# Moving the buffers of a four-layer matmul kernel to other SBUF addresses

## The reference, cut to what matters

```python
proj = h @ w_in                 # layer 1: 1024 x 10240, layer 2: 1024 x 4096
return y @ w_out                # 1024 x 1024
proj = x @ w_in                 # hybrid mixers: 1024 x 7256
merged @ w_out + b_out
u = x @ w_up                    # 1024 x 5632
(jax.nn.gelu(a) * b) @ w_down   # 2816 x 1024
```

## The kernel before

| buffer | start, byte | start modulo 512 |
|---|---|---|
| UT | 16512 | 128 |
| WS, and each slot and part in it | 49280 + 8192 n | 128 |
| WR | 98432 | 128 |
| CT | 114816 | 128 |
| SM | 118464 | 192 |
| AT, AF | 121536 | 192 |
| AR | 154304 | 192 |
| EX, EA | 205504 | 192 |
| MF | 222912 | 192 |

## Time and profile before

### The profile page before, as it was taken

One profiled execution on the slowest core, in us unless ns is written; L12 is line 12 of the kernel. 1 busy time (PEld: TensorE's weight loads), 2 busy tenths in 40 slices (PEclk: granted clock), 3 DMA queues, 4 the chain that ended last, 5 costly groups with the idle time before them and its releaser, 6 DMA issues.

```text
span 2716.8 us, 36054 instructions
## 1 busy us (share of the span) xinstructions
PE 2677.7 (99%) x13721; PEld 2153.6 (79%) x13721; DVE 1219.1 (45%) x2468; ACT 1049.5 (39%) x2005; POOL 1139.0 (42%) x894
## 2 busy tenths in 40 slices
PE   8999999999999999999999999999999999999998
PEld 6888888897778877776788888887777678888887
DVE  4434334443555456544246424265644423642426
ACT  3333434443446343452333424234445333342422
POOL 4434344435342443333365444444333336444443
PEclk9999999999999999999999999999999999999999
DMA  6444343432331332224252333324222425233331
GB/s 191 130 116 124 98 125 97 130 125 86 109 94 55 112 97 78 78 82 134 100 182 72 116 93 95 99 79 130 81 68 88 136 93 175 83 118 100 93 93 63
DMA packets 215056, 286.39 MB, mean 105 GB/s; under 512 B 16862, under 2 KB 154562, under 8 KB 214116
## 3 DMA queue, kind: packets, MB, share of 16 engines
q1 hardware_dynamic: 214884, 284.08, 34.2%
HBM read 248.31 MB, written 18.94 MB: 98 GB/s over the span
## 4 chain that ended last, share of the span: by engine, by line
PE 96%; DVE 2%; ACT 1%; POOL 1%; issue 1%; DMA 0%; ACTq 0%; DVEq 0%; POOLq 0%
PE banks L1687 39%; PE banks L1684 29%; PE banks L1680 13%; PE banks L1818 2%; PE banks L1705 2%; PE banks L1744 1%; PE banks L1800 1%; PE banks L1904 1%; PE banks L1720 1%; PE banks L1927 1%; PE banks L1839 1%; PE banks L1977 1%; PE banks L1861 1%; PE banks L1890 1%; PE banks L1786 1%; PE banks L1915 1%
## 5 line engine op out<-in xcount | busy, mean ns | idle before, releaser
L2991 POOL TENSOR_TENSOR WS<-WR,WS 128x512 fp32r<-128x512 f32 (+2 forms) x676 | 856.3, 1300 | 1048.6 <-ACT WS L2040 1048.6
L1687 PE MATMUL banks<-WS,UT 128*128 128x512 f32 (+1 forms) x3696 | 797.0, 365 | 3.9 <-DVE UT L2393 3.9
L1687 PEld LDWEIGHTS banks<-WS,UT 128*128 128x128 f32 x3696 | 605.8, 190 | 131.4 <-issue 36.4
L1684 PE MATMUL banks<-UT,WS 128*128 128x512 f32 (+1 forms) x2832 | 660.8, 392 | 0.7 <-ACT AR L2222 0.7
L1684 PEld LDWEIGHTS banks<-UT,WS 128*128 128x128 f32 (+1 forms) x2832 | 526.0, 187 | 125.8 <-issue 16.0
L2040 ACT ACTIVATE WS<-WR 128x1024 fp32r<-128x1024 f32 (+1 forms) x344 | 333.1, 1018 | 221.4 <-PE banks L1687 144.3
L1680 PE MATMUL banks<-UT,WS 128*128 128x512 f32 x1536 | 371.1, 395 | 0.0
L1680 PEld LDWEIGHTS banks<-UT,WS 128*128 128x128 f32 x1536 | 282.5, 188 | 61.9 <-issue 4.9
L1687 PE MATMUL banks<-WS,AT 128*128 128x512 f32 x1296 | 308.5, 396 | 0.0
L1687 PEld LDWEIGHTS banks<-WS,AT 128*128 128x128 f32 x1296 | 242.4, 188 | 58.2 <-ACT WS L2040 0.7
L2989 POOL TENSOR_TENSOR WS<-WR,WS 128x512 fp32r<-128x512 f32 x128 | 177.9, 1422 | 251.6 <-ACT WS L2036 251.6
(11 more groups left out here) (226 smaller groups left out, 2665.2 us busy)
## 6 DMA issues: line engine op xcount, KB each, us to landing
WR<-in_w_in SPq DMA_DIRECT2D x112, 512.0 KB, 3.6
WR<-in_w_up SPq DMA_DIRECT2D x88, 512.0 KB, 3.5
WR<-in_dil_w_in SPq DMA_DIRECT2D x64, 512.0 KB, 3.8
WR<-in_w_down SPq DMA_DIRECT2D x40, 512.0 KB, 3.7
WR<-in_diff_w_in SPq DMA_DIRECT2D x32, 512.0 KB, 3.8
WR<-in_dil_w_in SPq DMA_DIRECT2D x32, 256.0 KB, 3.2
AR<-AF SPq DMA_DIRECT2D x128, 64.0 KB, 2.3
AR<-AF SPq DMA_DIRECT2D x64, 128.0 KB, 2.4
```

Source lines behind the costliest of these rows:

```text
L1684: mm = pe.matmul(B[bank][0:c, :], w[part][:, kk, g * P:g * P + c], act[:, other, kk, :], start=start, stop=stop)
L1687: mm = pe.matmul(B[bank][:, off:off + n], act[:, other, before_k + kk, g * P:g * P + P], w[part][:, kk, :], start=start, stop=stop)
L2991: ge.tensor_tensor(slot(i, 1)[:, s], raw(i)[:, s], slot(i, 0)[:, s].bitcast(F32), ALU.subtract).then_inc(lo_p.sem, 1)
```

## The change

Four things move; no instruction is added, removed or reordered.

1. The slots of `WS` grow from 4096 to 4096 + 128 elements (512 bytes more).
2. The arena with `AT`, `AR`, `MF` and `EX` comes directly behind `WR`, ahead of `CT` and `SM`. `AR` starts 128 elements later behind `AT` than before, and shrinks from 17152 to 17008 elements (its last tables, `oSIN` and `oCOS`, move down by 144).
3. `slot` adds `lead(i)` to the start of a tile: 112 elements (448 bytes) for `l1w?`, `l1g?` and `l2g?`, 16 elements (64 bytes) for `f?a0`, `f?b0` and `f?b10`, and 0 for all others.
4. Tiles in `AT` are addressed through `AW`, the same bytes with 16 elements more.

| buffer | start after, byte | start modulo 512 before | after |
|---|---|---|---|
| UT, WR | 16512, 99968 | 128 | 128 |
| WS slots | 49280 + 16896 n | 128 | 128 |
| WS, tiles l1w, l1g, l2g | 448 further | 128 | 64 |
| WS, tiles f?b10 | 64 further | 128 | 192 |
| AT and AF | 116352 | 192 | 128 |
| AT, tiles f?a0 and f?b0 | 64 further | 192 | 192 |
| AR | 149632 | 192 | 128 |
| EX, EA | 200832 | 192 | 128 |
| MF | 217664 | 192 | 64 |
| CT | 222304 | 128 | 96 |
| SM | 225952 | 192 | 160 |

```diff
-        WS = sb("WS", [P, NS, 2, KC * 256], F32R)
+        WS = sb("WS", [P, NS, 4096 + 128], F32R)
         WR = sb("WR", [P, 2, KC * 256])
+
+        AR_LEN, EXT = 17008, 12800
+        o_ar = 4 * (8192 + 128)
+        base = -(-nc.sbuf_base // 32) * 32
+        sb("arena", [P, 8192 + 128 + AR_LEN + 1152 + 8])
         CT = sb("CT", [P, C_TAB])
         SM = sb("SM", [P, 768])
-
-        base = -(-nc.sbuf_base // 32) * 32
-        sb("arena", [P, 8192 + 17152 + 1152 + 8])
-        EXT = 12800
         AT = nc.alloc_sbuf_tensor_at("AT", [P, 2, KC, T], F32R, offset=base)
+        AW = nc.alloc_sbuf_tensor_at("AW", [P, 2 * KC * T + 16], F32R, offset=base)
         AF = nc.alloc_sbuf_tensor_at("AF", [P, 2 * KC * T], F32, offset=base)
-        AR = nc.alloc_sbuf_tensor_at("AR", [P, 17152], F32, offset=base + 32768)
-        MF = nc.alloc_sbuf_tensor_at("MF", [P, 1152], F32, offset=base + 32768 + 68608)
-        EX = nc.alloc_sbuf_tensor_at("EX", [P, 2, KC * 256], F32R, offset=base + 32768 + 4 * EXT)
-        EA = nc.alloc_sbuf_tensor_at("EA", [P, 2, 4, T], F32R, offset=base + 32768 + 4 * EXT)
+        AR = nc.alloc_sbuf_tensor_at("AR", [P, AR_LEN], F32, offset=base + o_ar)
+        MF = nc.alloc_sbuf_tensor_at("MF", [P, 1152], F32, offset=base + o_ar + 4 * AR_LEN)
+        EX = nc.alloc_sbuf_tensor_at("EX", [P, 2, KC * 256], F32R, offset=base + o_ar + 4 * EXT)
+        EA = nc.alloc_sbuf_tensor_at("EA", [P, 2, 4, T], F32R, offset=base + o_ar + 4 * EXT)
...
-        oSIN, oCOS = 17088, 17120
+        oSIN, oCOS = 16944, 16976
...
+        def lead(i):
+            name = tiles[i][0]
+            if name[:3] in ("l1w", "l1g", "l2g"):
+                return 112
+            return 16 if place[i] > NS or name[2:] == "b10" else 0
+
         def slot(i, part):
             _, k, n, _ = tiles[i]
             s = place[i]
+            o = 2048 * part + lead(i)
             if s < NS:
-                return WS[:, s, part, 0:k * n]
+                return WS[:, s, o:o + k * n]
             if s > NS:
-                return AT[:, s - NS - 1].rearrange("p k t -> p (k t)")[:, part * 2048:part * 2048 + k * n]
+                o += 4096 * (s - NS - 1)
+                return AW[:, o:o + k * n]
             return EX[:, part, 0:k * n]
```

## The result

| | before | after |
|---|---|---|
| median, 6 runs each | 2717.52 us (2716.45 to 2718.52) | 2708.11 us (2705.81 to 2709.33) |
| profiled execution (span) | 2718.07 us (2716.8) | 2707.59 us (2706.3) |
| mean granted clock in it | 0.999 | 0.998 |

The ratio of the times is 0.9963, with a 95% interval of 0.9952 to 0.9974: the change gains 9.4 us, where 16.0 us were forecast. Lines of the changed kernel are 12 further than those of the earlier trace rows: 1687 is 1699, 1684 is 1696, 1680 is 1692, 1705 is 1717, 1720 is 1732.

What follows compares the result with a forecast made beforehand. TensorE's matmul spacings were taken to bound the kernel, a matmul running in 99% of the span. Gains of 5.1, 3.1, 1.4, 0.5, 4.7 and 1.2 summed to 16.0 us, predicting 2701.4 us, range 2697.5 to 2709.5.

Steps and rivals of the forecast that it cites:

- d: Moving operand's start minus the stationary one's, modulo 512 bytes; claimed to set matmul spacing: 512 columns 226.7 ns at 0, 233.3 at -64.
- addresses do nothing: Rival for the whole kernel: the paces come from something other than operand place, time stays 2717.4 us; chance 0.05.
- (a): Four pieces of 192 matmuls (f?d0, f?d1), WS moving, AT stationary: 233.3 to 226.7 ns each, gaining 5.1 us.
- (b): Output projections of layers 1 and 2 and last down projection, AT stationary, WS or EX moving: gain of 3.1 us.
- (d): 96 matmuls with EX moving and UT stationary go from d = +64 to 0: gain of 0.5 us.
- (c): Line 1684 with AT or EA moving, 576 matmuls, goes from d = +64 to 0: gain of 1.4 us.
- (e): Tiles l1w, l1g, l2g, 1152 matmuls of 256 columns, go from d = 0 to -64: gain of 4.7 us.
- (f): Tiles f?b10, 192 matmuls of line 1720, take the pace of line 1705: gain of 1.2 us.
- (g): Tiles f?a0 and f?b0 keep their pair of starts, 128 and 192, so nothing changes.
- its rival, that the tiles gain nothing: Start values, not d, decide for l1w, l1g, l2g: 2706.1 us, or 2713 with mirrored loss; chance 0.12.
- (h): About 890 transposes go from d = -64 to -32: taken as 0, ends 4 us loss and 1 us gain.
- (i): Other engines keep their work and none bounds; TensorE gains at most 6% in a stretch; no time counted.

Runs made afterwards that it cites:

- scan1: Matmul-only kernel, not the reference: 16 differences of operand start in steps of 32 bytes; 512 columns took 226.7 ns at d = 0, 233.3 at -64.
- scan3: Matmul-only kernel with stationary operands of 128, 64 and 32 columns, either operand moved; 512 columns at d = 0 took 226.7, 230.0 and 231.6 ns.
- scan4: Matmul-only kernel: both operands shifted together, loads of 16 columns and 1 column, moving start in 16-byte steps; 226.65 ns unshifted, 239.4 shifted 4 bytes.
- arena_only: Changed kernel without the leads for l1w, l1g, l2g and f?b10; 2710.42 us, ratio 0.9976 to the kernel before.
- d76: Changed kernel with tables starting at 64 modulo 512 and leads making d = -76 for tiles used with 256 columns; 2712.86 us, ratio 0.9983.
- scan2: Matmul-only kernel: 64 differences of operand start, -128 to +124 bytes in steps of 4; 512 columns took 226.7 to about 240.3 ns.

## Why the prediction was right and wrong

**What bounds the kernel, and that d separates the pairs: right.** `scan1` shows both paces with no other engine at work, and that at 512 columns the difference and not the values decides on the 64-byte grid. The rival "addresses do nothing" is out, and with it, for these matmuls, the rule of the Trainium skill, "SBUF — State Buffer", section "Who interferes with whom", that "PE and ACT never wait on anyone", as far as TensorE's two own reads are concerned: 226.7 against 233.3 ns and -8.1 us in the kernel. The other rule that the prediction quoted, "TensorE: Matmul & The Clock Gate", section "Step-by-step: what each phase is for", by which the load takes nothing from the stream, is not borne out either: in `scan3` what d = -64 costs falls from 6.7 to 2.7 ns with a load half as wide, and in `scan4`, with a load of one column, the stationary start no longer counts. That only bits below 512 count was right for the steady pace at 512 columns, and too wide: on the 64-byte grid 256 is enough.

**(a) and (b), 8.2 us forecast, -8.1 us measured in `WS`,`AT`.** The size was right; one piece of the working in (b) was not. `EX` and `AT` both started at 192 before, so the 144 matmuls of that pair had d = 0 already and had nothing to gain. It cost nothing in the sum, since the short pieces gained 5.7 ns each (528 matmuls, 3.0 us) where I had allowed 2.9. The reading behind that allowance was wrong too: the piece of 96 at 1411 us had 229.6 ns not for being short but for the pair of part (d) in it, and had 21.77/96 = 226.8 ns after the change. Two errors cancelled here.

**(c) and (d), right**: -1.3 and -0.4 us for 1.4 and 0.5.

**(e), (f) and (g): here the main step failed, in that d = -64 at 256 columns was given one pace.** It has two, 117.8 and 113.3 ns, and a run keeps the one with which it begins. The trace of before showed it, in a row that I didn't use: the first run of line 1705 in the same view as the earlier trace rows, 24 matmuls, stood at 117.9 ns.

```profile
1457.12 2.83 PE banks L1705 x24
```

I read the pace off the two runs of 48 and gave it to `l1w0` ("10.9 us as well"), to `f?b10` ("exactly the pair of line 1705") and to line 1705 itself ("Nothing"). Measured: `l1w0` 11.31 us for 96, `f?b10` 22.61/192 = 117.8 ns, and both 48s of line 1717 flipped from the fast pace to the slow one, +0.8 us. That is the sign of being wrong that the prediction had named, a changed pace of a pair whose d did not change. (e) came to 3.7 of 4.7 us: the 96 of `l1w0` gained 2.1 ns each, the 732 matmuls in runs of 12 2.6 ns, and those in runs of 24 to 60 4.4 to 6.2 ns; 0.9 of the 3.7 us came without the leads (`arena_only`). (f) came to 0.4 of 1.2; (g) to -0.8 of 0. Together 2.6 us of the shortfall. Neither bound of (e) was reached, and its rival, that the tiles gain nothing, fell: the leads alone gave -2.9 us.

**(h), right.** Eight transposes still take 0.87 us; `scan1` has 109.2 ns at every d. Both rivals by which the transposes themselves pay are out. What comes behind them did pay: line 1717's flip stands in `arena_only`, which moved their operands.

**(i), wrong in kind, small in size.** "TensorE gains at most 6% in a stretch" was no argument against a wait, because this stage had no slack at all: from the first matmul of `f?b10` to the late tile it takes 18.6 us in seven kernels. The prediction looked at TensorE's longest waits alone; the weight loads' idle time of 0.7 us behind "ACT WS" stood in the trace of before. It does name that sign. The wait costs what `f?b10` gained, 0.3 of 0.4 us here and 1.2 of 1.2 us in `d76`. So (f) was worth nothing however fast it became.

**Not in the sum**: one more stretch of half clock, 1.7 us, and 0.7 us of other waits. The six executions give 2705.81 us at a mean clock of 0.999 and up to 2709.33 at 0.997. The clock varies from execution to execution, but a mean of 0.998 or less was more frequent with moved addresses (28 of 55 executions, against 5 of 44 of the kernel before), so it is not scatter alone, and the forecast had no term for it.

**The time and its range.** The median, 2708.11 us, lies 6.7 us above the forecast and within the range of 2697.5 to 2709.5 us. That is partly luck: the high end was made for gate tiles that gain nothing and transposes that pay, and neither came. Two paces at one d, the wait and the clock filled the room in their place, and none of them had a price in the forecast.

In all, by the rows of the table of groups: 16.0 forecast, less 0.3 in (a) to (d), 1.0 (e), 0.8 (f), 0.8 (g), 0.3 (the wait), 1.7 (clock) and 1.4 (other waits and what is unassigned), makes 9.7 us.

**Open.** What chooses between 117.8 and 113.3 ns; why the mean clock was lower more often with the moved addresses; and why a moving operand on the 64-byte grid has 226.7 ns beside a full load and 231.3 ns beside a load of one column. No version was clearly faster than the changed kernel.

## What to carry to other kernels

Where TensorE is the bound, put moving and stationary fp32r operands of 512 columns at the same start modulo 256 bytes, and every moving start on the 64-byte grid: that part of this change held everywhere, 6.7 ns per matmul against d = -64, with no instruction touched. Read a pace from every run of a line and not from the most frequent one: two paces of one pair in the same view mean that the entry counts, and then a gain is worth its slower pace. A pace that matmuls alone hold behind every entry tried need not hold in the kernel, as `d76` showed. And before a faster stretch is counted, look how far behind the next split or load ends: a stage whose sum stays the same in seven versions gives back what TensorE gains in it.

## What the runs showed of the hardware that was not expected

- The place of the operands within 64 bytes counts besides d: at d = 0 and 512 columns 226.65, 239.4, 233.35 and 230.0 ns for 0, 4, 8 and 16 bytes. With a load of one column 36 bytes of the moving start cost 7 ns (238.3 against 231.3 ns) and 36 bytes of the stationary start nothing. Over all starts tried in steps of 4 bytes the cost was between nothing and 13.7 ns.
- A full weight load beside the stream can be faster than a small one: 226.7 ns with 128 columns, 231.6 ns with 32, both at d = 0.
- The best d depends on the columns: 0 is among the fastest at 512 columns (226.7 ns) and among the slower ones at 256 (120.0 ns), where -76 by the stationary start ran at 113.3 ns in `scan2` and `scan3`, but at 113.3 and at 120.0 ns in the kernel.
- The same 48 matmuls at the same addresses run steadily at 117.8 or at 113.3 ns, with nothing different but what ran before them.
